# A transformer block pair in float32: the down products' weight sums move from VectorE to accumulating DMAs issued by GpSimd

## What is computed

```python
# first block
h2 = _rmsnorm(x, norm2_w) * (1.0 + scale2) + shift2
ffn = jnp.dot(jax.nn.silu(jnp.dot(h2, w_ffn_gate)) * jnp.dot(h2, w_ffn_up), w_ffn_down)
x = x + gate2 * ffn
# second block
u = causal_dwconv(rms_norm(h, ffn_norm[l]) @ w_up[l], conv_w[l], conv_b[l])
gate, up = jnp.split(u, 2, axis=-1)
h = h + (jax.nn.silu(gate) * up) @ w_down[l]
```

## Time and profile before

| | us |
|---|---|
| median of 2 runs | 1522.67 (1522.29 to 1523.06) |
| span of the profiled execution | 1520.9 |
| TensorE busy | 1499.2 (99%) |
| VectorE busy | 1026.8 (68%) |
| ScalarE busy | 661.2 (43%) |
| GpSimd busy | 46.2 (3%) |
| DMA, mean | 151 GB/s |

### The profile page before, as it was taken

The page is one execution under the profiler, slowest core; times in us unless marked ns, Lnnn a source line. Parts: engine busy times, 40 slices in busy tenths (PEclk is TensorE's granted clock), DMA queues, the critical chain, the costliest instruction groups (busy, mean ns, idle before and its releaser), DMA issues.

```text
span 1520.9 us, 21091 instructions
## 1 busy us (share of the span) xinstructions
PE 1499.2 (99%) x8527; PEld 1224.3 (80%) x8527; DVE 1026.8 (68%) x1773; ACT 661.2 (43%) x1090; POOL 46.2 (3%) x82
## 2 busy tenths in 40 slices
PE   7999999999999999999999999999999999999999
PEld 5777888778888898888888777777788988888887
DVE  6679886766588666444459876787567456556885
ACT  4453334653222342222246553766525434434653
POOL 0000000000000000000000021200011000000000
PEclk9999999999999999999999999999999999999999
DMA  9423122149778457665535515100113232232473
GB/s 385 146 83 97 56 70 84 57 181 343 271 267 307 153 187 285 233 222 200 201 127 184 180 60 222 56 30 29 57 56 129 93 107 85 86 111 97 135 229 128
DMA packets 77210, 229.29 MB, mean 151 GB/s; under 512 B 6453, under 2 KB 6581, under 8 KB 75961
## 3 DMA queue, kind: packets, MB, share of 16 engines
q1 hardware_dynamic: 77112, 227.94, 42.9%
HBM read 202.75 MB, written 25.17 MB: 150 GB/s over the span
## 4 chain that ended last, share of the span: by engine, by line
PE 91%; DVE 5%; ACT 3%; issue 1%; POOL 0%; DMA 0%; SPq 0%; DVEq 0%; ACTq 0%
PE bank L696 86%; PE bank L708 4%; DVE AR L1922 1%; DVE wl L1900 1%; ACT wh L1376 0%; DVE G L1929 0%; DVE AR L2232 0%; DVE X L1922 0%; DVE Hl L1922 0%; DVE X L1929 0%; ACT AR L1387 0%; DVE ST L1922 0%; DMA CST<-in_cst 0%; ACT AR L1399 0%; ACT AR L1774 0%
## 5 line engine op out<-in xcount | busy, mean ns | idle before, releaser
L1376 ACT ACTIVATE wh<-raw 128x1024 fp32r<-128x1024 f32 (+1 forms) x223 | 230.6, 1035 | 363.2 <-PE bank L696 317.7
L1900 DVE TENSOR_TENSOR wl<-raw,wh 128x1024 fp32r<-128x1024 f32 (+1 forms) x223 | 263.7, 1192 | 91.7 <-ACT wh L1376 91.6
L696 PE MATMUL bank<-wh,Hh 128*128 128x512 f32 (+1 forms) x726 | 293.1, 404 | 3.8 <-DVE wl L1900 2.5
L696 PE MATMUL bank<-wh,Hl 128*128 128x512 f32 (+1 forms) x726 | 281.1, 387 | 0.0
L696 PE MATMUL bank<-wl,Hh 128*128 128x512 f32 (+1 forms) x726 | 280.3, 386 | 0.0
L696 PE MATMUL bank<-Hh,wh 128*128 128x512 f32 (+2 forms) x712 | 268.5, 377 | 0.2
L696 PE MATMUL bank<-Hl,wh 128*128 128x512 f32 (+2 forms) x712 | 266.9, 375 | 0.0
L696 PE MATMUL bank<-Hh,wl 128*128 128x512 f32 (+2 forms) x712 | 266.9, 375 | 0.0
L696 PEld LDWEIGHTS bank<-wh,Hh 128*128 128x128 f32 x726 | 136.5, 188 | 38.6 <-issue 9.7
L696 PEld LDWEIGHTS bank<-wh,Hl 128*128 128x128 f32 x726 | 136.3, 188 | 28.5
L696 PEld LDWEIGHTS bank<-wl,Hh 128*128 128x128 f32 x726 | 136.8, 188 | 23.4
(11 more groups left out here) (271 smaller groups left out, 2022.2 us busy)
## 6 DMA issues: line engine op xcount, KB each, us to landing
raw<-in_wst SPq DMA_DIRECT2D x224, 512.0 KB, 4.2
CST<-in_down SPq DMA_DIRECT2D x22, 1024.0 KB, 5.9
sums_dram<-CST SPq DMA_DIRECT2D x22, 1024.0 KB, 4.8
raw<-sums_dram SPq DMA_DIRECT2D x40, 512.0 KB, 3.9
raw<-in_down SPq DMA_DIRECT2D x30, 512.0 KB, 3.6
AR<-in_wst SPq DMA_DIRECT2D x8, 1024.0 KB, 11.3
X<-in_x SPq DMA_DIRECT2D x8, 512.0 KB, 6.0
AR<-in_wst SPq DMA_DIRECT2D x5, 512.0 KB, 5.3
```

The source lines that it names most:

```text
L696: return e.matmul(o, l, r, start=start, stop=stop, skip_group_check=True)
L1376: e.activation(HI[slot[i]][:, 0:width(i)], raw[:, i % NR, 0:width(i)], ACT.Copy).then_inc(*w_hi.mark(i))
L1900: e.tensor_tensor(LO[slot[i]][:, 0:n], raw[:, i % NR, 0:n], HI[slot[i]][:, 0:n].bitcast(f32), SUB).then_inc(*w_lo.mark(i))
```

## The change

The four sums are no longer computed by VectorE. GpSimd issues DMAs that load a quarter into a half of `SUMT` and other DMAs that add a further quarter to what is there (`accum_op=ADD`), and stores the half after each step. Two pairs are done at a time (`PAIRS`: five groups of two pairs and one of one pair per product, twelve groups in all). The adding DMAs only add, so the sums have other signs: "7" is b22+b12, "5" is b12+b11, "6" is "5" plus b22, and "4" is "6" plus b21. The left sums and the places where the products are added are given signs to match (`left_sum`, `added`, `add_product`). The number of VectorE's instructions there stays the same. In GpSimd's program the six groups of `dn` and the first two of `2dn` stand ahead of the four `n2` roots, the other four groups behind them. `summing` and the steps of SyncE and VectorE that it placed are gone. VectorE waits, ahead of zeroing the edges of `FULL`, until all sums are stored.

```diff
-def summing(ticks):
...
-    for among, every, after in ((early, 12, 6), (late, 10 / 3, 2)):
...
+PAIRS = [(0, 1), (2, 3), (4, 5), (6, 7), (8, 9), (10,)]
...
+        def summed(key, u):
+            return 6 * SEVEN.index(key) + u
...
         def stored(key, p):
-            return s_sums, 16 * (11 * SEVEN.index(key) + p + 1)
+            return s_sums, 64 * (summed(key, min(p // 2, 5)) + 1)
...
-            def right_sums(key, p):
-                b11, b12, b21, b22 = (SUMT[:, 512 * q:512 * q + 512] for q in range(4))
-                on.wait_ge(*pair_in(key, p))
-                tt(b22, b22, b12, SUB)
-                own()
-                tt(b12, b12, b11, SUB)
-                tt(b11, b11, b22, ADD)
-                own()
-                tt(b21, b21, b11, SUB, ("right sums", key, p))
-            w = Weave(ticks, lambda k: [[consume(i) for i in done_at[k]], [right_sums(*pair) for pair in pair_sum_at[k]]])
+            w = Weave(ticks, lambda k: [consume(i) for i in done_at[k]])
...
-                a, b = {"6": (group("4", u), group("7", u)), "5": (group("1", u), group("6", u)), "3": (group("2", u), group("6", u))}[z]
-                tt(group(z, u), a, b, ADD if z == "5" else SUB, (key, "left sum", z, u))
+                if z == "6":
+                    stt(group(z, u), group("7", u), -1.0, group("4", u), MUL, SUB, (key, "left sum", z, u))
+                else:
+                    tt(group(z, u), group({"5": "1", "3": "2"}[z], u), group("6", u), ADD, (key, "left sum", z, u))
...
+            on.wait_ge(*stored("2dn", 10))
             for n in "kv":
                 for g in (0, 1):
                     e.memset(FULL[n][:, :, g, 31:32], 0.0).then_inc(*dve.mark(*[("pads",)] * ((n, g) == ("v", 1))))
...
-                tt(xs, xs, bank[BANKS[z][r]][:, :], ADD, ("2dn", event, r))
+                tt(xs, xs, bank[BANKS[z][r]][:, :], SUB if z in "76" and n == 1 else ADD, ("2dn", event, r))
...
         def pool_program(e, on):
+            def right_sums(key, u):
+                ps, g = PAIRS[u], summed(key, u)
+                n, m = len(ps), SEVEN.index(key)
+                t1, t3 = (SUMT[:, o:o + 512 * n].rearrange("p (k c) -> p k c", k=n) for o in (0, 1024))
+                quarters = down_in[m].rearrange("(a q p) (h c) -> q h p a c", q=2, p=P, h=2)[:, :, :, ps[0]:ps[-1] + 1, :]
+                def store(z, t):
+                    e.dma_start(sums_dram[m, SUMMED.index(z), ps[0]:ps[-1] + 1].rearrange("a p c -> p a c"), t).then_inc(s_sums, 16)
+                if g == 0:
+                    on.wait_ge(*dve.of(("inner", T - 1, 1)))
+                else:
+                    on.wait_ge(s_sums, 64 * g)
+                e.dma_start(t3, quarters[1, 1]).then_inc(s_halves, 16)
+                e.dma_start(t1, quarters[0, 1]).then_inc(s_halves, 16)
+                on.wait_ge(s_halves, 32 * (g + 1))
+                e.dma_start(t3, quarters[0, 1], accum_op=ADD).then_inc(s_added, 16)
+                e.dma_start(t1, quarters[0, 0], accum_op=ADD).then_inc(s_added, 16)
+                on.wait_ge(s_added, 64 * g + 32)
+                store("7", t3)
+                store("5", t1)
+                on.wait_ge(s_sums, 64 * g + 32)
+                e.dma_start(t1, quarters[1, 1], accum_op=ADD).then_inc(s_added, 16)
+                on.wait_ge(s_added, 64 * g + 48)
+                store("6", t1)
+                on.wait_ge(s_sums, 64 * g + 48)
+                e.dma_start(t1, quarters[1, 0], accum_op=ADD).then_inc(s_added, 16)
+                on.wait_ge(s_added, 64 * g + 64)
+                store("4", t1)
...
+            for u in range(6):
+                right_sums("dn", u)
+            for u in (0, 1):
+                right_sums("2dn", u)
             for t in range(T):
                 root(ST[:, 16 + t:17 + t], act.of(("n2", "mean", t)), ("n2", "root", t))
+            for u in (2, 3, 4, 5):
+                right_sums("2dn", u)
...
-            def pair_load(key, p):
...
-            def pair_store(key, p):
...
-            w = Weave(ticks, lambda k: [[load(i) for i in load_at[k]], [pair_store(*pair) for pair in pair_store_at[k]], [pair_load(*pair) for pair in pair_load_at[k]]])
+            w = Weave(ticks, lambda k: [load(i) for i in load_at[k]])
```

More of the change, by code:

```diff
@@ L127, in seven_order @@
     return [(s, *step) for s, step in enumerate(steps)]
-EARLY = ("ga0", "ga1", "gb0", "gb1", "ap0", "ap1", "rp0", "rp1", "wo0")
+PAIRS = [(0, 1), (2, 3), (4, 5), (6, 7), (8, 9), (10,)]
 def seven_parts(key):
     return [(key + z, g, None, 0, 1 if g == 5 else 2, [(0, 512)]) for _, z, g, rows in seven_order() if 0 in rows]
-def summing(ticks):
[L142 to L145, removed]
-    for among, every, after in ((early, 12, 6), (late, 10 / 3, 2)):
[L147 to L155, removed]
 class Count:
@@ L360, in program @@
     place, ticks, hi_at, done_at, load_at, slot, before = schedule(chunks)
-    pair_load_at, pair_sum_at, pair_store_at = summing(ticks)
     widths = [c[4] * sum(n for _, n in c[5]) for c in chunks]
@@ L418, in program @@
         s_cst, s_cst2, s_prm, s_bc, s_out = (sem(n) for n in ("s_cst", "s_cst2", "s_prm", "s_bc", "s_out"))
-        s_pair, s_sums = sem("s_pair"), sem("s_sums")
+        s_halves, s_added, s_sums = sem("s_halves"), sem("s_added"), sem("s_sums")
         s_in = [sem(f"s_in{t}") for t in range(T)]
@@ L603, in program @@
         SUMS_AT = {2: ("6", 0), 4: ("6", 1), 6: ("6", 2), 8: ("5", 0), 9: ("5", 1), 10: ("5", 2), 12: ("3", 0), 14: ("3", 1), 16: ("3", 2)}
+        def summed(key, u):
+            return 6 * SEVEN.index(key) + u
         def stored(key, p):
-            return s_sums, 16 * (11 * SEVEN.index(key) + p + 1)
-        def pair_in(key, p):
-            return s_pair, 16 * (11 * SEVEN.index(key) + p + 1)
+            return s_sums, 64 * (summed(key, min(p // 2, 5)) + 1)
         def group(z, u):
@@ L2443, in added @@
                 on.wait_ge(*dense.of(("dn", z, r)))
-                tt(to, a, bank[BANKS[z][r]][:, :], ADD, ("dn", event, r))
+                b = bank[BANKS[z][r]][:, :]
+                if z in "53":
+                    tt(to, b, a, SUB, ("dn", event, r))
+                else:
+                    tt(to, a, b, ADD, ("dn", event, r))
             for s, z, g, rows in w.steps("dn"):
@@ L2457, in vector_program @@
                         on.wait_ge(*act.of(("dn", "u", r)))
-                        tt(SGR[2 + r], SGR[2 + r], SGR[r], ADD)
+                        tt(SGR[2 + r], SGR[2 + r], SGR[r], SUB)
                         gated(SGR[2 + r], 1, 2 + r)
@@ L2860, in load @@
                 e.dma_start(part_of_raw(i), stream(i)).then_inc(s_raw[i % NR], 16)
-            def pair_load(key, p):
[L2863 to L2867, removed]
-            def pair_store(key, p):
-                on.wait_ge(*dve.of(("right sums", key, p)))
-                e.dma_start(sums_dram[SEVEN.index(key), :, p].rearrange("q p c -> p q c"), SUMT.rearrange("p (q c) -> p q c", q=4)).then_inc(s_sums, 16)
             FINISHED = {24: ("c11", (0, 1), 0, 0), 38: ("c22", (0, 1), 1, 1), 41: ("c12", (0, 1), 0, 1), 46: ("c21", (0,), 1, 0), 47: ("c21", (1,), 1, 0)}
-            w = Weave(ticks, lambda k: [[load(i) for i in load_at[k]], [pair_store(*pair) for pair in pair_store_at[k]], [pair_load(*pair) for pair in pair_load_at[k]]])
+            w = Weave(ticks, lambda k: [load(i) for i in load_at[k]])
             def row(g):
```

## The result

The changed kernel takes 1604.5 us (1600.4 and 1608.7, two runs) against 1522.7 us: 1.054 times the time, 95% interval 1.047 to 1.060. The forecast was 1523 us, its range ended at 1585; the result is rival (a), a late chain at the n2 roots, and it lies beyond the range. The profiled execution of the changed kernel is the slower of the two, 1608.7 us.

The account below looks back on a forecast made before the run. TensorE was taken as the bound, busy 1499.2 of 1520.9 us. With 0 removed and 0 to 1 us added, 1521 us, plus 1.8 for the median of the runs, gave 1523 us; range 1519 to 1585.

Parts of the forecast that it names:

- rival (a): At the n2 roots: GpSimd's chain of sums ends late and TensorE stalls; 1562 us with adding doubled; chance 0.42.
- VectorE's relief: In the sums' stretches: 58.8 us less VectorE work, covered by TensorE; gain 0 to 0.2 us, taken as 0.
- the slack at the n2 root: At the first n2 root: it may be about 0.4 us late; beyond that a stall of the same size.
- The later dates: Behind the roots: the remaining groups end near 665 us, more than 200 us before the dates at 872.3 and 895.0; cost nothing.
- 0.67 us for each of the 80 DMAs: Chain ahead of the n2 roots: 54.0 us spare in 279.6 us of room; an extra of this size makes it late.
- I take 0, since the reads of the destination and of HBM could run side by side: Adding DMAs in GpSimd's chain: adding costs nothing over a plain transfer; taken as 0 us.
- the upper price: Adding DMAs in GpSimd's chain: bytes count twice, 7.1 us a group, 52.9 us ahead of the roots.
- I cost the crowding at 0.: DMA engines beside the weight loads: room on the mean; 0, or a microsecond or two where a weight lands late.
- rival (b): Crowded DMA engines make weights late at TensorE: 3 to 15 us, 1526 to 1538 us; chance 0.05.
- Issue by GpSimd: GpSimd's chain ahead of the roots: 0.5 us for each of 80 DMAs, 40 us.
- the forecast's landings: Seven full groups and a half one ahead of the roots, transfers only, adding and issue free: 225.6 us.
- Its line with doubled adding and 1.0 us more per DMA: Late chain at the n2 roots, adding doubled and 1.0 us per issue in place of 0.5: 1601 us.

Follow-up runs that it names:

- seven groups: The changed kernel with seven groups of sums ahead of the n2 roots on GpSimd's queue and five behind, in place of eight and four: 1563.5 us, ratio 1.027.

## Why the prediction was wrong

The reading of what bounds the kernel held: TensorE was the bound, VectorE's relief is worth nothing (shown by the run without its operations), the slack at the n2 root is next to none and a late root costs its own size (eight against seven groups). The later dates were met, and VectorE's busy time fell to 972.1 us against 968 forecast. The decision between the forecast and rival (a), "0.67 us for each of the 80 DMAs", was the right question. The extra came to (363.3 - 225.6) / 80 = 1.72 us per DMA. What failed is the answer, in two terms of the sum, both set to nothing:

- **"I take 0, since the reads of the destination and of HBM could run side by side".** Adding was not free. The run without adding puts the term at 59.7 us of the chain between the profiled executions and at 51.3 us of time between the medians, and the rates of 207 against 400 GB/s fit with it: the upper price, bytes counted twice, gave 52.9 us. The rule that I weighed and set aside, from the Trainium skill, "Collectives: The Full Stack", section "The bandwidth ceiling: the fold count and why AG ≠ RS ≠ AR", says it of ReduceScatter against AllGather, 32.35 against 62.28 GB/s; this trace agrees: half the rate. That two reads are the reason is the page's account, and no run here shows it. An adding DMA also holds GpSimd for 1.2 us where a plain one takes 0.73; what that adds to the chain is not separated.
- **"I cost the crowding at 0."** I asked there only whether weights would be late for TensorE, and that was nearly right (1.8 us, less than rival (b) had). I did not ask what the weight loads do to the chain. The medians that I took were not low for the stretch: the eleven pair loads of 1 MB from 326 to 520 us landed in 6.0 us (4.8 to 7.9) before. But SyncE had issued them, in the queue of the weight loads. From GpSimd's queue two loads of the same 1 MB took 8.8, 9.2 and 7.2 us in the third to fifth groups, from start to next start. Whether the second queue or only the added traffic makes the difference was not tested. Halving the weights' bytes gave the chain back 27.4 us, and groups beside the full loads took 57 us against 38.5 us alone.

**"Issue by GpSimd"**, "I take 0.5 us", 40 us in all, was no cause of the miss. Without adding, a group between 275.8 and 309.4 us took 33.7 us against 29.8, so 0.4 us for each of its ten DMAs, 29 us or so for 7.5 groups (this includes what little crowding there was: before the change the DMA engines were 15% busy there). By the quiet stages it is less: two loads 5.4 us, counted twice, two stores 5.1, a load 4.3 and a store 3.5, twice each, are 31.5 us, 13 us over the forecast for 7.5 groups.

The sum with what was measured: of the 363.3 us at which the root started (239.9 to 603.2), 225.6 were the forecast's landings and 59.7 are adding. That leaves 78 us for GpSimd's issues and the crowding together. With 13 to 29 us for the issues the crowding is 49 to 65 us. Two readings fit with that: half of the weights' bytes is worth 27.4 us, and the first five groups took 259.4 us together where five quiet ones take 192.5.

Rival (a) at 1562 us had adding doubled and no crowding of the chain. Its line with doubled adding and 1.0 us more per DMA gave 1601 us, close to the 1604.5 measured, since 78 us are 0.97 for each of the 80 DMAs. That is luck in part: the 1.0 us was a price of GpSimd's issue, and most of the 78 us is crowding, which stands in none of rival (a)'s sums. The bound of 1585 left that line out, because it asked for two dear prices together; nothing tied them to be cheap. And the remark that 2% is about what a measurement of this kernel can tell from no change was too coarse: ten runs each told 3 us, 0.2%, from nothing.

## What to carry to other kernels

Work that an engine does inside another's shadow is free, and moving it buys nothing; ask first what the queue that takes it over must still deliver on time. Here four roots of under 1 us each were placed behind a chain of 80 transfers. A chain of dependent DMAs costs its landings one by one, an adding transfer cost twice its bytes here, and a landing measured alone or on another queue does not give its price beside other loads; put the short, dated work of a queue ahead of such a chain, or leave the chain a margin larger than its own spread from run to run.

## What the runs showed of the hardware

- An adding DMA from HBM into SBUF ran at about 205 GB/s against 375 to 410 for a copy of the same shape, with the engines as busy, and its 512 KB landed 5.6 us after issue in a quiet stretch, a copy's 4.0 us.
- GpSimd's issue of a plain DMA of 128x2x512 took 0.73 us and of an adding one 1.2 us; two adding ones took 2.49 us from the start of the first record to the end of the second (535.03 to 537.52 us), two plain ones 1.44 (529.62 to 531.06).
- After the stall TensorE did not come back at full speed. It had idled 81.7 us, and the granted clock, 1.00 up to 526 us, was 0.82 from 526 to 530 us and 0.50 from 530 us on, the level of 1.2 GHz; it stayed there for the first microseconds of work. In the chain after (start, us, what) the first eight transposes take 1.97 us and the next twelve matmuls 4.48:

```profile
604.95 1.97 PE bank L688 x8
606.92 4.48 PE bank L676 x12
```

against 0.87 and 2.77 us for the same pieces in the chain before:

```profile
521.74 0.87 PE bank L708 x8
522.61 2.77 PE bank L696 x12
```

That is 2.8 us on top of the wait. The granted clock is the column before the last two:

```profile
604.00:608.00 4.00, 3.05 (x12) 2.76 (x13) 1.76 (x3) 1.81 (x5) 1.47 (x3) 0.50 0.27 101
608.00:614.00 6.00, 6.00 (x27) 4.94 (x26) 3.90 (x7) 4.12 (x9) 0.00 (x0) 0.79 0.01 1
614.00:622.00 8.00, 8.00 (x54) 7.19 (x53) 7.88 (x11) 5.72 (x10) 1.58 (x4) 1.00 0.39 133
```
